# Second block of a two-block transformer in split float32: the norm's shift as a high and a low column of the high stream, the third product on 256 columns, the two result columns added by GpSimd

## What is computed

```python
h = rms_norm(x, ln1_g[l]) * (1.0 + sc1) + sh1
z = h @ w_in[l]
u_pool, c_q_raw, c_kv_raw, k_rope_raw, gz_a, gz_b = jnp.split(z, cuts, axis=-1)
...
merged = jax.nn.sigmoid(gz_a) * y_a + jax.nn.sigmoid(gz_b) * y_b
x = x + g1 * (merged @ w_out[l])

h2 = rms_norm(x, ln2_g[l]) * (1.0 + sc2) + sh2
x = x + g2 * (jnp.square(jax.nn.relu(h2 @ w_ff1[l])) @ w_ff2[l])
```

## Time and profile before

| what | value |
|---|---|
| median of three runs | 1832.86 us (1832.69 to 1833.85) |
| the profiled execution | 1833.77 us, span 1832.4 us |
| PE busy | 1818.7 us (99%) |
| PEld busy | 1785.8 us (97%) |
| DVE busy | 1369.0 us (75%) |
| ACT busy | 1046.1 us (57%) |
| POOL busy | 3.1 us, 9 instructions |
| DMA | 365 MB, 199 GB/s in the mean |

### The profile page before, as it was taken

One profiled execution on the slowest core, in us unless ns is written; L12 is line 12 of the kernel. 1 busy time (PEld: TensorE's weight loads), 2 busy tenths in 40 slices (PEclk: granted clock), 3 DMA queues, 4 the chain that ended last, 5 costly groups with the idle time before them and its releaser, 6 DMA issues.

```text
span 1832.4 us, 36084 instructions
## 1 busy us (share of the span) xinstructions
PE 1818.7 (99%) x15071; PEld 1785.8 (97%) x15071; DVE 1369.0 (75%) x2356; ACT 1046.1 (57%) x1730; POOL 3.1 (0%) x9
## 2 busy tenths in 40 slices
PE   9999999999999999999999999999999999999998
PEld 8999999999999999999899999999999999999998
DVE  6887786677876788778667887797877559778754
ACT  6454675665444544458656554675665457656633
POOL 0000000000000000000000000000000000000000
PEclk9999999999999999999999999999999999999999
DMA  8876432457784677544346786454555554455553
GB/s 280 314 277 233 139 139 93 139 197 257 267 299 173 231 263 284 213 139 138 116 162 234 285 295 247 139 179 161 175 182 185 193 177 166 155 180 186 185 184 115
DMA packets 52386, 365.32 MB, mean 199 GB/s; under 512 B 6684, under 2 KB 7356, under 8 KB 10880
## 3 DMA queue, kind: packets, MB, share of 16 engines
q1 hardware_dynamic: 51792, 362.23, 55.9%
q10 hardware_dynamic: 432, 0.79, 0.1%
HBM read 361.94 MB, written 1.05 MB: 198 GB/s over the span
## 4 chain that ended last, share of the span: by engine, by line
PE 88%; DVE 7%; ACT 2%; DMA 2%; issue 1%; SPq 0%; DVEq 0%; ACTq 0%
PE bank L562 26%; PE bank L563 26%; PE bank L564 26%; DVE w_lo L1750 2%; PE bank L622 1%; PE bank L619 1%; PE bank L618 1%; ACT w_hi L1193 1%; PE bank L844 1%; PE bank L859 1%; DMA raw_b<-in_weights 1%; PE bank L889 0%; DMA c_rows<-in_c_rows 0%; DMA ada_raw<-in_ada_w 0%; DVE s_pool L2266 0%
## 5 line engine op out<-in xcount | busy, mean ns | idle before, releaser
L562 PE MATMUL bank<-xn_hi,w_hi 128*128 128x272 f32 (+2 forms) x2640 | 758.3, 287 | 0.8 <-DVE w_lo L1750 0.8
L564 PE MATMUL bank<-xn_lo,w_hi 128*128 128x272 f32 (+2 forms) x2640 | 749.1, 284 | 0.0
L563 PE MATMUL bank<-xn_hi,w_lo 128*128 128x272 f32 (+2 forms) x2640 | 748.9, 284 | 0.0
L562 PEld LDWEIGHTS bank<-xn_hi,w_hi 128*128 128x128 f32 x2640 | 498.2, 189 | 7.8 <-issue 5.8
L563 PEld LDWEIGHTS bank<-xn_hi,w_lo 128*128 128x128 f32 x2640 | 498.2, 189 | 0.8
L564 PEld LDWEIGHTS bank<-xn_lo,w_hi 128*128 128x128 f32 x2640 | 498.2, 189 | 0.0
L1193 ACT ACTIVATE w_hi<-raw_a 128x1024 fp32r<-128x1024 f32 (+2 forms) x278 | 303.2, 1091 | 278.7 <-PE bank L564 242.3
L1193 ACT ACTIVATE w_hi<-raw_b 128x1024 fp32r<-128x1024 f32 (+2 forms) x280 | 305.7, 1092 | 264.6 <-PE bank L564 235.6
L1750 DVE TENSOR_TENSOR w_lo<-raw_b,w_hi 128x1024 fp32r<-128x1024 f32 (+2 forms) x280 | 354.0, 1264 | 133.4 <-ACT w_hi L1193 131.1
L1750 DVE TENSOR_TENSOR w_lo<-raw_a,w_hi 128x1024 fp32r<-128x1024 f32 (+1 forms) x276 | 350.1, 1269 | 124.3 <-ACT w_hi L1193 122.9
L562 PE MATMUL bank<-h_hi,w_hi 128*128 128x272 f32 (+1 forms) x704 | 200.8, 285 | 0.1
(11 more groups left out here) (358 smaller groups left out, 2649.8 us busy)
## 6 DMA issues: line engine op xcount, KB each, us to landing
raw_b<-in_weights SPq DMA_DIRECT2D x122, 1024.0 KB, 4.8
raw_a<-in_weights SPq DMA_DIRECT2D x121, 1024.0 KB, 4.8
ada_raw<-in_ada_w SPq DMA_DIRECT2D x48, 1024.0 KB, 5.0
raw_a<-in_weights SPq DMA_DIRECT2D x16, 1408.0 KB, 5.8
raw_b<-in_weights SPq DMA_DIRECT2D x16, 1408.0 KB, 5.9
c_rows<-in_c_rows SPq DMA_DIRECT2D x3, 512.0 KB, 6.1
raw_b<-in_weights SPq DMA_DIRECT2D x2, 768.0 KB, 4.1
raw_a<-in_weights SPq DMA_DIRECT2D x2, 640.0 KB, 3.9
```

The source lines that it names most:

```text
L562: pe.matmul(o, wh, xh, start=start, stop=False)
L563: pe.matmul(o, wl, xh, start=False, stop=False)
L564: return pe.matmul(o, wh, xl, start=False, stop=stop)
```

## The change

The two further columns now both stand in the high stream: column 256 is the rounded shift, column 257 the rest. The half is gone, and the low stream has no further columns. The products on `xn_hi` stay on 258 columns; the one on `xn_lo` runs on the 256 tokens. `product` is called no more at these places: a new `shifted_product` issues high by high (258), low input by high weight (256), high input by low weight (258). The result columns 256 and 257 are `sh_hi @ w` and `sh_lo @ w`; GpSimd adds them in place, for the gates also times 0.5, and ACT waits for that (semaphore `shifted`) instead of DVE's `tile_v`. PE's banks are still released by `tile_v`. `shift_column` is one ACT and one DVE instruction now, in place of two each.

```diff
+def low_cols(cols):
+    return TN if cols == TX else cols
...
+    def whole_shift(tile, key, scale=None):
+        pool.wait_ge(*k.at("tile_v", key))
+        o, rest = tile[:, N:N + 1], tile[:, N + 1:N + 2]
+        if scale:
+            pool.tensor_scalar(o, o, rest, scale, ALU.add, ALU.mult).then_inc(*k.up("shifted", key))
+        else:
+            pool.tensor_tensor(o, o, rest, ALU.add).then_inc(*k.up("shifted", key))
+
+    for l in range(L):
+        for at in range(31):
+            if is_moved(at):
+                whole_shift(mixed_tile(c, at), ("n2", l, at), 0.5 if at > 9 else None)
+        for n in range(KF2):
+            whole_shift(f_of(c, n, TX), ("ff1", l, n))
...
+    def shifted_product(b, wh, wl, xh, xl, kk, ready=None):
+        pe.matmul(b[:, TX], wh, stream(xh, kk, TX), start=kk == 0, stop=False)
+        if ready:
+            pe.wait_ge(*ready)
+        pe.matmul(b[:, TN], wh, stream(xl, kk, TN), start=False, stop=False)
+        return pe.matmul(b[:, TX], wl, stream(xh, kk, TX), start=False, stop=kk == KD - 1)
...
-        return pe.matmul(b[0:LR, cols], both[:, 0:LR], stream(xl, kk, cols), start=False, stop=kk == KD - 1, skip_group_check=True)
+        part = low_cols(cols)
+        return pe.matmul(b[0:LR, part], both[:, 0:LR], stream(xl, kk, part), start=False, stop=kk == KD - 1, skip_group_check=True)
...
-        for i, part in enumerate((1.0, 0.5)):
-            act.activation(hi.tile[:, :, hi.at + N + i], c.mod_all[:, l, first:first + 8], ACT.Copy, scale=part).then_inc(*k.up("x_hi", ("shift", l, first, i)))
+        act.activation(hi.tile[:, :, hi.at + N], c.mod_all[:, l, first:first + 8], ACT.Copy).then_inc(*k.up("x_hi", ("shift", l, first)))
...
             if is_moved(at):
-                act.wait_ge(*k.at("tile_v", ("n2", l, at)))
+                act.wait_ge(*k.at("shifted", ("n2", l, at)))
...
-            act.wait_ge(*k.at("tile_v", ("ff1", l, n)))
+            act.wait_ge(*k.at("shifted", ("ff1", l, n)))
...
+        dve.tensor_tensor(hi.tile[:, :, hi.at + N + 1], c.mod_all[:, l, first:first + 8], hi.tile[:, :, hi.at + N].bitcast(F32), ALU.subtract).then_inc(
+            *k.up("x_lo", ("shift", l, first)))
```

More of the change, by code:

```diff
@@ L170 @@
     "w_lo", "piece_lo", "x_lo", "scaled", "tile_v", "sums", "gla_v", "att_v", "ada_v", "rope_v", "mod_v", "fn_v", "gated",
-    "cleared", "pooled", "last_scaled",
+    "cleared", "pooled", "last_scaled", "shifted",
 ]
@@ L360, in gate_of, with mixed_tile @@
     return at - 10 if at < 12 else at - 14 if at < 22 else at - 15
+def mixed_tile(c, at):
+    if at < 3:
+        return c.cq_x[:, at, :]
+    if at < 5:
+        return c.ckv_x[:, at - 3, :]
+    if at == 5:
+        return c.full[0:64, 1, TX]
+    return c.u_pool[:, at - 6, META:T + 2] if at < 10 else c.gates2_x[:, gate_of(at), :]
 def f_of(c, n, cols=TN):
@@ L584, in tile @@
             s = slice(kk * rows, (kk + 1) * rows)
-            m = product(bank[b][0:rows, cols], wh[:, s], wl[:, s], stream(xh, kk, cols), stream(xl, kk, cols), kk == 0, kk == k_tiles - 1)
+            if cols == TX:
+                m = shifted_product(bank[b], wh[:, s], wl[:, s], xh, xl, kk)
+            else:
+                m = product(bank[b][0:rows, cols], wh[:, s], wl[:, s], stream(xh, kk, cols), stream(xl, kk, cols), kk == 0, kk == k_tiles - 1)
         end_unit(u, m)
@@ L616, in tiles_as_ready @@
             for b, (wh, wl) in enumerate((wa, wb)):
-                o = bank[b0 + b][:, cols]
-                pe.matmul(o, wh[:, s], stream(xh, kk, cols), start=kk == 0, stop=False)
-                pe.matmul(o, wl[:, s], stream(xh, kk, cols), start=False, stop=False)
-                if b == 0:
-                    pe.wait_ge(*k.at("x_lo", (*stage, kk)))
-                m = pe.matmul(o, wh[:, s], stream(xl, kk, cols), start=False, stop=kk == KD - 1)
+                if cols == TX:
+                    m = shifted_product(bank[b0 + b], wh[:, s], wl[:, s], xh, xl, kk, k.at("x_lo", (*stage, kk)) if b == 0 else None)
+                else:
+                    o = bank[b0 + b][:, cols]
+                    pe.matmul(o, wh[:, s], stream(xh, kk, cols), start=kk == 0, stop=False)
+                    pe.matmul(o, wl[:, s], stream(xh, kk, cols), start=False, stop=False)
+                    if b == 0:
+                        pe.wait_ge(*k.at("x_lo", (*stage, kk)))
+                    m = pe.matmul(o, wh[:, s], stream(xl, kk, cols), start=False, stop=kk == KD - 1)
                 if kk == KD - 1:
@@ L1643, in mixer2 @@
                     j = gate_of(at)
-                    act.activation(c.gates2[:, j, :], c.gates2[:, j, :], ACT.Tanh, bias=c.gates2_x[:, j, N + 1:N + 2], scale=0.5).then_inc(*k.up("tile_a", ("gate", l, j)))
+                    act.activation(c.gates2[:, j, :], c.gates2[:, j, :], ACT.Tanh, bias=c.gates2_x[:, j, N:N + 1], scale=0.5).then_inc(*k.up("tile_a", ("gate", l, j)))
                 if 22 < at < 27:
@@ L1842, in shift_column @@
     def shift_column(l, first):
-        hi, lo = streams(c, ("ff" if first else "ln1", l))
-        for i, part in enumerate((1.0, 0.5)):
-            dve.wait_ge(*k.at("x_hi", ("shift", l, first, i)))
-            dve.scalar_tensor_tensor(out=lo.tile[:, :, lo.at + N + i], in0=c.mod_all[:, l, first:first + 8], scalar=part, in1=hi.tile[:, :, hi.at + N + i].bitcast(F32),
-                                     op0=ALU.mult, op1=ALU.subtract).then_inc(*k.up("x_lo", ("shift", l, first, i)))
+        hi = streams(c, ("ff" if first else "ln1", l))[0]
+        dve.wait_ge(*k.at("x_hi", ("shift", l, first)))
+        dve.tensor_tensor(hi.tile[:, :, hi.at + N + 1], c.mod_all[:, l, first:first + 8], hi.tile[:, :, hi.at + N].bitcast(F32), ALU.subtract).then_inc(
+            *k.up("x_lo", ("shift", l, first)))
     def gains(l):
@@ L2313, in mixer2 @@
             finish(chains, at)
-            if at < 5:
-                scaled_tile(u, c.cq_x[:, at, :] if at < 3 else c.ckv_x[:, at - 3, :], moved_bank(at), ("n2", l, at))
-            elif at == 5:
-                scaled_tile(u, c.full[0:64, 1, TX], 5, ("n2", l, at), rows=64)
-            elif at < 10:
-                scaled_tile(u, c.u_pool[:, at - 6, META:T + 2], moved_bank(at), ("n2", l, at))
-            elif is_moved(at):
-                scaled_tile(u, c.gates2_x[:, gate_of(at), :], moved_bank(at), ("n2", l, at))
+            if is_moved(at):
+                scaled_tile(u, mixed_tile(c, at), moved_bank(at), ("n2", l, at), rows=64 if at == 5 else P)
             if l == 0 and 26 < at < 31:
```

## The result

| | before | after |
|---|---|---|
| median of six runs each, taken beside each other | 1832.84 us (1832.69 to 1834.42) | 1842.43 us (1841.4 to 1843.49) |
| ratio, 95% interval | | 1.005 (1.004 to 1.0061) |
| the profiled execution | 1833.77 us, span 1832.4 us | 1842.74 us, span 1841.4 us |

The changed kernel is 9.6 us slower. The forecast was no change, 1832.7 us with 1835.2 as the upper end, so it is wrong in time and in sign. Where the time went is read from the ends of the units' last matmuls in the two traces. A stretch here runs from the end of a stage's first unit to the end of the next stage's first unit; the mixer is cut in two at the end of the first unit behind its last gate unit.

The account below looks back on a forecast made before the run. PE bounds the kernel, VectorE part of the second block's mixer. -3.0 - 0.05 + 0.05 + 0.53 + 2.4 = -0.1 us from the 1832.86 median gave 1832.7 us, no change, range 1830.2 to 1835.2.

Parts of the forecast that it names:

- The part that saves: Second block: 912 third products cut from 258 to 256 columns, 3.3 ns each, 3.0 us, plus 0.05 from rotary-key units.
- the pitch of 256 is not reached: Rival: 256 columns between two of 258 doesn't reach the 256 pitch; saving only 0.9 us, total 1834.6 us; chance 0.06.
- What costs nothing on PE: Turned product order and the wait for `xn_lo` one product earlier cost nothing; 0.5 us if the cover were gone.
- GpSimd's taking turns: GpSimd waits for VectorE's running two-SBUF-input instruction, VectorE's next waits for GpSimd; mixer loses 1.2 us a layer.
- The sign that I gave: Check in the profile: PE's wait before the attention's first transposition grows from 0.36 to some 1.8 us in both layers.
- What PE saves ahead of this place is lost at it: Mixer: PE's saving is lost waiting for VectorE at the stretch's end, 0.27 us a layer, 0.53 in both.
- the step of `u_pool`: Mixer, layer 0, 1189.48: ScalarE's shift addition starts 0.3 us later behind GpSimd, and VectorE waits all 0.3 longer.
- The hold of 0.1 us: GpSimd's addition of one column holds about 0.1 us, between 0.1 and 1.1, taken nearest to a 98 ns write.
- a long add: Rival: twenty mixer adds each hold VectorE, up to 2 us per further 0.1 us; 1840.7 at 0.5 us; chance 0.15.
- one Tanh of two: Attention's start: ScalarE's Tanh 1.2 us later behind a weight split, VectorE's reciprocal and PE's transposition 0.6 us late.
- some three that make VectorE wait 0.1 us each: Mixer: the other GpSimd adds in the VectorE-bound stretch, together 0.3 us in a layer.
- The feed-forward product hides the additions: First feed-forward product: low weights are ready 6.1 us before PE starts, so GpSimd waits of 0.4 to 1.2 us stay hidden.

Follow-up runs that it names:

- e2: Kernel before with only the third product of each k-step on 256 columns, old order, nothing on GpSimd: 1837.74 us, ratio 1.0021.
- e4: Changed kernel without GpSimd's additions, ScalarE waiting for VectorE's scaling again: 1838.59 us, ratio 1.0029.
- e1: Kernel before with only the order of the three products turned, all on 258 columns, nothing on GpSimd: 1833.35 us, ratio 0.9995.
- e7: Kernel before with the third product on 256 columns, old order, xn_lo at 0, 48, 32 and 40 floats in the four stages: 1830.79 us, one run.
- e3: Kernel before, products unchanged, with a GpSimd addition put between VectorE's scaling and ScalarE's step: 1838.53 us, ratio 1.0026.
- e11: Kernel before with the change in the feed-forward product alone, xn_lo there at 48 floats: 1830.36 us, ratio 0.9984.
- e8: Kernel before with GpSimd between VectorE and ScalarE, only writing a zero to the spare column instead of adding: 1833.6 us, ratio 0.9998.
- e6: Changed kernel's products without GpSimd's additions, both xn_hi and xn_lo moved to other places in their rows in each stage: 1836.92 us, one run.

## Why the prediction was wrong

**The part that saves (-3.05 us): wrong in size and sign.** I took the pace of a product of 256 columns from a stage in which all products have 256, and added it to two of 258. These runs show that a product's pace isn't its own; it depends on what streams beside it and on where the streams begin. With the places as they stood the term is +1.6 us in each feed-forward product and some 0.6 a layer in the mixer, 3.9 us by e2's median, where I had -3.05; in the changed kernel's order it is +1.6 in each feed-forward product, 0.7 behind the first of them, and 0.5 and 0.3 in the mixer (e4). My rival "the pitch of 256 is not reached" came near with the right remark, that no row shows the two widths in turn, but it still let the change save 0.9 us. Nothing in the trace excluded a loss, and I gave none a chance. At better places the term is -1.6 us a feed-forward product, twice the 0.84 I had forecast.

What I held against that rival, that the pitch holds in every stage with one width, isn't so in the trace of the kernel before. The product on `y` at the end of the mixer has 256 columns throughout, and in its two layers it runs so (four k-steps apart):

```profile
1296.35 0.28 PE L562 MATMUL bank<-y_hi,w_hi 128*128 128x256 f32 x1
...
1297.76 0.28 PE L562 MATMUL bank<-y_hi,w_hi 128*128 128x256 f32 x1
...
1626.77 0.28 PE L562 MATMUL bank<-y_hi,w_hi 128*128 128x256 f32 x1
...
1628.17 0.28 PE L562 MATMUL bank<-y_hi,w_hi 128*128 128x256 f32 x1
```

That is 1.41 us in layer 0 and 1.40 in layer 1; over six units of each, 353.3 and 350.0 ns a k-step. Two paces at one width were there to be read. The formula on the Trainium skill's page "TensorE: Matmul & The Clock Gate" (Back-to-back issue gap), which the page gives for a single isolated matmul, goes by columns alone; here the pace differs at equal columns, and the measurement decides.

**What costs nothing on PE: right.** The turned order and the earlier wait for `xn_lo` moved nothing (e1).

**GpSimd's taking turns: right in the main, in half of the working.** An addition does wait for the running VectorE instruction with two SBUF inputs, and lasts 1.17 us at the very split that I named. The other half, that VectorE's next instruction waits for GpSimd, doesn't show in the mixer: its instructions there last as long as before. The Tanh starts 1.47 us later in its chain (a wait of 2.19 for 0.72), and PE waits 1.09 us ahead of the first transposition for 0.20 before. That is 0.9 us more, where the sum had 0.6. The sign that I gave, some 1.8 us in all, was too large: counted as its 0.36 was, from start to start, it is 1.25. What PE saves ahead of this place is lost at it, as I had said: in e7, layer 1, PE is 0.28 us ahead of before in front of it and 0.06 behind it. At 1189.47 the step of `u_pool` is late by 0.23 us and `ckv_lo` waits 0.34 longer, for which I had 0.3.

**The hold of 0.1 us: wrong.** I took it from a write, and the row that decides is the one on reading: the fastest addition takes 194 ns, the gates' 267, the median one 0.3 to 0.4. But that isn't what cost most. My rival "a long add", with its price of 2 us for each 0.1 us, doesn't hold either: VectorE's instructions didn't get longer. That its 1840.7 us for adds of 0.5 us lies near the measured time is chance.

**The step that failed in the mixer: I followed one Tanh of two, and the leads of one stage.** Of the gates ahead of the queries I looked at none, though the unit before the queries has the same arrangement as the one that I worked out, an addition just ahead of a weight split. There it costs 0.94 us, since `p_hi`, for which VectorE waits, stands behind that Tanh on ScalarE. The rotary key's addition, behind three `cq` instructions, costs 0.67. I priced both with "some three that make VectorE wait 0.1 us each". And I read the lead of the low weights only in the feed-forward product (6.1 us). In the mixer it is a tenth of that. VectorE's split for the unit behind the value product, and PE's start on it, in the kernel before:

```profile
1209.78 1.23 DVE L1750 TENSOR_TENSOR w_lo<-raw_a,w_hi 128x1024 fp32r<-128x1024 f32 x1
...
1211.64 0.28 PE L562 MATMUL bank<-xn_hi,w_hi 128*128 128x258 f32 x1
```

1211.64 - 1211.01 = 0.63 us. VectorE lost 1.95 us ahead of it, so PE came to wait for weights, which the prediction named as what would make it wrong. Per layer the mixer lost 2.7 us by the hop (e3), for which I had 1.2. (The sum's own terms come to -0.07, so to 1832.8 us and not 1832.7; nothing hangs on that.)

**The feed-forward product hides the additions: right** (e3: +0.02 / -0.02; e11: no loss).

## What to carry to other kernels

Columns that are cut from one of several products that run in turn need not save anything, and here they cost 3.9 us: look at the distance of the starts over the whole group after the change, and if it grew, move the place at which the streams begin before giving the change up. A small step on an idle engine cost nothing here where it only wrote (e8), but one that reads SBUF beside a busy VectorE ended only when VectorE let it, up to 1.5 us later, and what it costs is to be followed along the order of the engine that waits for it, at every place where such a step stands ahead of a long VectorE instruction. A lead of weights that hides a wait in one stage says nothing on another; read it in each stage that the change touches.

## What was not expected of the hardware

- The same matmuls on the same operands run at 353.3 or at 366.7 ns for three, and keep the one or the other over whole stages. The stage behind, with other operands, can run slower as well, 0.7 us in the changed kernel and 2.5 us in e6. What switches the paces wasn't settled; in the changed kernel these products change theirs only where other matmuls come between.
- Moving one stream by 8 float32 in its row (56 to 48) makes a k-step of 258, 256 and 258 columns go from 366.7 to 353.3 ns, and one of three times 258 from 360.0 to 362.5.
- A two-operand addition of one column on GpSimd takes 0.19 to 0.3 us when VectorE leaves it through, and up to 1.5 us behind VectorE, while a write of one column takes 98 ns at the same places.
